# One decode-and-prompt step of a four-mixer trunk: the samples' state outputs as eight full matmuls a layer in place of 32 quarter ones

## What is computed

```python
def step(s, inp):
    u_, wk_, qk_, qh_, kt_, gl_ = inp
    w = u_ - jnp.einsum('bhcd,bhde->bhce', wk_, s)
    o = jnp.einsum('bhcd,bhde->bhce', qh_, s) + jnp.einsum('bhij,bhje->bhie', qk_, w)
    s = jnp.exp(gl_)[..., None, None] * s + jnp.einsum('bhcd,bhce->bhde', kt_, w)
    return s, o
```

## Time and profile before

| | us |
|---|---|
| runs of the kernel before | 1393.62, 1399.95, 1400.35 |
| median | 1399.95 |
| profiled execution | 1395.48 |
| span of its profile | 1393.7 |
| TensorE busy in it | 1273.7 (91%) |
| VectorE busy | 922.9 (66%) |
| ScalarE busy | 730.6 (52%) |
| mean granted TensorE clock | 0.932 of full |

### The profile page before, as it was taken

The page is one execution under the profiler, slowest core; times in us unless marked ns, Lnnn a source line. Parts: engine busy times, 40 slices in busy tenths (PEclk is TensorE's granted clock), DMA queues, the critical chain, the costliest instruction groups (busy, mean ns, idle before and its releaser), DMA issues.

```text
span 1393.7 us, 24010 instructions
## 1 busy us (share of the span) xinstructions
PE 1273.7 (91%) x9815; PEld 1086.3 (78%) x9815; DVE 922.9 (66%) x1546; ACT 730.6 (52%) x1190; POOL 10.0 (1%) x22
## 2 busy tenths in 40 slices
PE   4999898887999998998898788999999999999994
PEld 3899756666999997998666556788878887888874
DVE  1674635724555545676457437998899799979995
ACT  2567222204444444573122115887778778877772
POOL 0000000000000000000000000000000000000000
PEclk8999968698999999999866799999999999999998
DMA  9535358653443453456265431998899889979980
GB/s 388 232 146 208 128 186 327 213 215 121 182 182 144 167 190 129 178 181 219 61 231 183 182 121 61 337 389 306 317 343 386 308 318 346 378 285 337 367 347 33
DMA packets 30325, 326.66 MB, mean 234 GB/s; under 512 B 6018, under 2 KB 6530, under 8 KB 8066
## 3 DMA queue, kind: packets, MB, share of 16 engines
q1 hardware_dynamic: 28738, 319.17, 61.1%
q0 software_dynamic: 1472, 5.89, 1.1%
HBM read 319.15 MB, written 5.89 MB: 233 GB/s over the span
## 4 chain that ended last, share of the span: by engine, by line
PE 82%; DVE 9%; DMA 3%; ACT 3%; issue 3%; SPq 0%; DVEq 0%; POOL 0%; ACTq 0%; POOLq 0%
PE bank L751 19%; PE bank L752 18%; PE bank L753 18%; PE bank L1136 4%; DMA ring<-in_w_ada 3%; PE bank L671 3%; PE bank L807 2%; PE bank L1230 2%; PE bank L703 1%; PE bank L648 1%; PE bank L1258 1%; DVE low L1902 1%; PE bank L693 1%; PE bank L774 1%; PE bank L1009 1%
## 5 line engine op out<-in xcount | busy, mean ns | idle before, releaser
L2425 DVE TENSOR_TENSOR low<-ring,w_high 128x1024 fp32r<-128x1024 f32 x352 | 401.7, 1172 | 41.7 <-ACT w_high L1777 32.9
L1777 ACT ACTIVATE w_high<-ring 128x1024 fp32r<-128x1024 f32 x352 | 355.3, 1021 | 50.5 <-PE bank L753 49.9
L751 PE MATMUL bank<-w_high,hcH 128*128 128x512 f32 x448 | 178.1, 398 | 1.5 <-DVE low L2425 1.3
L753 PE MATMUL bank<-low,hcH 128*128 128x512 f32 x448 | 175.3, 391 | 0.0
L752 PE MATMUL bank<-w_high,hcL 128*128 128x512 f32 x448 | 175.1, 391 | 0.0
L1399 ACT ACTIVATE arena<-bank 128x264 f32<-128x264 f32 (+8 forms) x128 | 51.7, 406 | 135.2 <-PE bank L648 53.9
L751 PE MATMUL bank<-pH,win_high 128*128 128x264 f32 x416 | 120.2, 289 | 2.5 <-issue 2.0
L752 PE MATMUL bank<-pH,low 128*128 128x264 f32 x416 | 118.1, 284 | 0.0
L753 PE MATMUL bank<-pL,win_high 128*128 128x264 f32 x416 | 117.9, 283 | 0.0
L751 PE MATMUL bank<-hH,w_high 128*128 128x264 f32 x352 | 101.1, 287 | 4.9 <-DVE low L2302 4.9
L1399 ACT ACTIVATE w_high<-ring 128x1024 fp32r<-128x1024 f32 (+1 forms) x76 | 71.5, 945 | 63.3 <-PE bank L753 63.3
(11 more groups left out here) (396 smaller groups left out, 2382.9 us busy)
## 6 DMA issues: line engine op xcount, KB each, us to landing
ring<-in_moe_gu SPq DMA_DIRECT2D x56, 2048.0 KB, 8.5
ring<-in_moe_down SPq DMA_DIRECT2D x32, 1792.0 KB, 7.9
ring<-in_w_ada SPq DMA_DIRECT2D x24, 2048.0 KB, 8.9
ring<-in_w_in SPq DMA_DIRECT2D x16, 1536.0 KB, 6.6
ring<-in_ffn_gu SPq DMA_DIRECT2D x11, 2048.0 KB, 7.9
ring<-in_ffn_down SPq DMA_DIRECT2D x8, 1408.0 KB, 5.9
ring<-in_w_out SPq DMA_DIRECT2D x4, 2048.0 KB, 8.3
ring<-in_cache_fox_k SPq DMA_DIRECT2D x32, 128.0 KB, 3.0
```

Source lines behind the costliest of these rows:

```text
L751: mm(out, wh, xh, start=start, stop=False)
L753: return mm(out, wh, xl, start=False, stop=stop)
L1777: A_(split(w_high), src, ACT.Copy).then_inc(sem("w_high_ready"), 1)
L2425: TT(piece_view(t, e_slot(e, i), ring_low)[0], src, split(w_high), ALU.subtract).then_inc(sem("w_low_ready"), 1)
```

## The change

A new tile `qm`, cleared once at the start, holds for each sample, each t and each of two halves a query column that is zero in the partitions of the other head. VectorE fills it with two copies a layer (`own_queries`, ahead of `delta_decay`). `state_outputs` then makes one call for each sample: both of the sample's tiles (128 partitions by 128 columns, four heads) are stationary, and its four query columns move. The result has four columns for each sample in bank 5, of which each head's own output stands in one half of the partitions of one column; ScalarE picks these out with four copies in place of one.

```diff
--- before.py
+++ after.py
@@ -229,6 +229,7 @@
         sxy = sb("sxy", [P, NS])
         rounds = sb("rounds", [P, 1], I32)
         mrow = sb("mrow", [P, P])
+        qm = sb("qm", [P, NS, 2, 2])
 
         ARENA = 25360
 
@@ -1002,12 +1003,8 @@
             def state_outputs():
                 o.need("gst_ready")
                 b = fill(5, "oTs_copied")
-                for t in range(2):
-                    for r in range(2):
-                        q = slice(r * HD, (r + 1) * HD)
-                        for i in range(NS):
-                            ins = mm(b[q, t * NS + i:t * NS + i + 1], gst[q, 2 * i + t, :],
-                                     act[q, t, SEQ + i:SEQ + i + 1], start=True, stop=True)
+                for i in range(NS):
+                    ins = mm(b[:, 4 * i:4 * i + 4], gst[:, 2 * i:2 * i + 2, :], qm[:, i, :, :], start=True, stop=True)
                 ins.then_inc(sem("oTs_done"), 1)
 
             def query_rows():
@@ -1653,7 +1650,11 @@
                                  "v_copied")
                     elif n == 5:
                         o.need("oTs_done")
-                        copy(oT[:, :, SEQ:NT], bank[5][:, 0:2 * NS].rearrange("p (t b) -> p t b", t=2), "oTs_copied")
+                        own = bank[5][:, 0:4 * NS].rearrange("p (b c) -> p c b", c=4)
+                        for t in range(2):
+                            for r in range(2):
+                                o.go(A_(oT[r * HD:(r + 1) * HD, t, SEQ:NT], own[t * HD:(t + 1) * HD, 2 * t + r, :],
+                                        ACT.Copy), "oTs_copied" if t + r == 2 else None)
                     elif n == 6:
                         o.need("yA_gated")
                         o.go(A_(sq[:, 0:2, :], yA[:, :, :], ACT.Square), "head_squares")
@@ -1820,6 +1821,7 @@
                 o.settle()
 
             vs(ve.memset(epsc[:, :], EPS))
+            vs(ve.memset(qm[:, :, :, :], 0.0))
             ve.wait_ge(sem("x_landed"), 16)
             vs(ve.memset(sq[:, 0, 0:1], 0.0), "x_whole")
 
@@ -2154,7 +2156,14 @@
                         v(STT(yA[:, t, SEQ:NT], act[:, 6 + t, SEQ:NT], dcol[:, l, t:t + 1],
                               yd16[:, :].rearrange("p (b t) -> p t b", t=2)[:, t, :], ALU.mult, ALU.add))
 
+                def own_queries():
+
+                    for r in range(2):
+                        q = slice(r * HD, (r + 1) * HD)
+                        v(CP(qm[q, :, :, r], act[q, 0:2, SEQ:NT].rearrange("p t b -> p b t")))
+
                 def delta_decay():
+                    own_queries()
                     vs(TT(g4, g4, spread_bt(2), ALU.mult), "tmpA_free")
                     kbc = act[:, 2:4, SEQ:NT].rearrange("p t b -> p b t").unsqueeze(3).broadcast_to([P, NS, 2, HD])
                     v(TT(b4, g4, kbc, ALU.mult), "Sk_ready")
```

## The result

Over 20 executions of each, the changed kernel took 1401.76 us in the median (1395.43 to 1409.99) and the kernel before 1397.1 us. The recorded ratio, an estimate of its own and not the quotient of the two medians (1.0033), is 1.0048, with a 95% interval of 1.0031 to 1.0064: slower by 4 to 9 us, where 2.9 us less were forecast, and outside the range given. Slow executions, more than 1.5% above the fastest of the same kernel (in the experiments five of the kernel before and one of another), are left out of every mean in this document. The profiled execution took 1401.70 us, its span 1399.9 us, and its mean granted clock was 0.928 (before: 1395.48, 1393.7 and 0.932).

What follows compares the result with a forecast made beforehand. TensorE was taken to bound the kernel, at 82% of the chain that ended last. Savings of 1.44 us (layer 0) and 1.46 us (layer 1), together 2.90, came off a base of 1397.7: 1394.8 us, range 1389 to 1400.5.

Steps and rivals of the forecast that it cites:

- the one on VectorE: VectorE's two copies per layer, 0.33 us, hidden in idle time, and one clearing at the start: no cost.
- The range's own terms: Whole time: 1391.4 to 1398.2, layer 0's bounds (0.2 down, 0.7 up), some 2 us spread each side.
- TensorE's term: State output block: 3.20 to 1.76 us in layer 0, 5.71 to 3.44 in layer 1; saves 1.44 and 1.46.
- the ceiling of 1.46 us: Layer 1: VectorE's idle time before the cache bias, taken as the most that a shorter block can save there.
- the sum: Both layers' savings on TensorE, 1.44 + 1.46 = 2.90 us, with nothing paid back elsewhere.
- The rival that the clock is lost further on: Layer 1 after the cache bias: extra TensorE idle keeps half clock, costing 3.36 us; 1398.2 us, chance 0.15.
- The winning rival: Layer 0 after the block: full clock stays up, saving 3.36 us more; 1391.4 us, chance 0.15.
- The overlap of quarters: State output block: by the skill's page four quarter matmuls cost about one full one, saving 0; the prediction went by the rows.
- The copies of VectorE and ScalarE: Around the block: VectorE's two, 0.33 us a layer, and ScalarE's four, at most 0.54 us more, fit in waits: nothing.

Runs made afterwards that it cites:

- the shift alone: Kernel before plus one unused tile of 128 bytes per partition where the change puts its query tile, no instruction differing; ratios 1.0066 and 1.0038 against the kernel before.
- Quarters in turn: Kernel before with two loops swapped in both layers, so consecutive quarter matmuls go to the two diagonal quarters alternately; ratios 1.0006 and 0.9992 against the kernel before.

## Why the prediction was wrong, point by point

- **The step that failed** is the one on VectorE: "The one clearing of the query tile stands at the start, ahead of VectorE's wait for the input: nothing." The tile was costed by its instructions alone, and no step asked what lies behind it in memory. It measured +6.55 us in the expert stage of the profile, and 7.2 us on the whole time (the shift alone). Without that term the forecast could not be right in sign. (The range's own terms add up to 1400.9 at the top, not 1400.5; 1401.76 lies above both.)
- **TensorE's term was right.** Forecast 1.76 us for the block in layer 0 at full clock, traced 1.88; 3.44 us at half clock, traced 3.6. Layer 1 was cut at the ceiling of 1.46 us, and its idle time went to nothing, with VectorE's passes over the first cache late next, as said. In layer 0 VectorE's idle time was to fall to about 2.6 us and fell to 0.60, since the clock stayed full behind the block.
- **That the sum arrives, "with nothing paid back", was wrong.** At equal half clock the change is worth 3.3 us at the old layout and 3.9 us at the moved one. But with the new block TensorE spends 11 to 17 us more at half clock, and with the tiles at their old places the kernel is level with the one before. The rival that the clock is lost further on had the mechanism, but one place and one price (3.36 us in layer 1, 0.15); that place did fall in the profile (19.58 us for 16.22). Over many executions the added half clock took, at 0.30 us for each, about all of the saving; where in the kernel it arises was not traced.
- **The winning rival** came true only in part: the clock stayed full up to 262 us in layer 0 and the bias came 4.23 us earlier. It had fallen at 268 us, and by 684 us nothing was left.
- **The overlap of quarters** was rightly not counted on for eight quarters in a row through one place. Quarters in turn do overlap (2.0 us), so the old block could be shortened without the change.
- **The copies of VectorE and ScalarE** cost nothing that shows. VectorE's two copies took 0.36 us a layer (0.33 forecast), and its wait before head 4's scores fell from 0.95 to 0.53 us in layer 0 and from 1.36 to 0.74 in layer 1, more than the "0.33 us and no more" that was put down. ScalarE's four copies took 0.76 us. In layer 0 they did not end before TensorE's transposes, as they should have: these ended at 250.92 + 0.38 = 251.30, and ScalarE's next copy came right behind the four, without its old wait of 0.62 us. TensorE did not wait for it.

```profile
250.96 0.76 ACT L1656 ACTIVATE arena<-bank 64x8 f32<-64x8 f32 x4 [1.56 <-PE bank L1007]
251.75 0.49 ACT L1396 ACTIVATE arena<-bank 128x384 f32<-128x384 f32 x1
```

What stays open is why the shorter block goes with more half clock. The amount of TensorE's work does not order the kernels (half clock above the kernel before beside them: 5.9 us with the block left out, 6.7 with half of it, 18.7 and 12.2 with the eight matmuls, 21.6 with them made twice), though with standard errors of 4 to 5 us no neighbours in this list are told apart. Which layer it comes from, and which property of the block decides, was not settled.

## What to carry to other kernels

A new tile is a change to every tile allocated behind it: read the start addresses of the hot operands before and after, and put a small tile where nothing lies behind it, or pad it so that the large ones keep their multiples of 256 bytes. Test such a change by moving the tiles alone, without its instructions; that run costs one line and separates layout from work. A saving of some us on a chain whose clock varies is to be weighed over many executions together with their granted clock, since one trace showed 4 us gained and then lost again in places that the change does not touch.

## What had not been expected of the hardware

- The start of an operand's tile within 256 bytes has a price on matmuls of 512 moving columns: 130.7 us for a pair of experts at a multiple of 256 or of 1024, 131.4 at 64 off, 132.5 at 128 off; 131.3 with the moving tile alone 128 off, and 132.7 with what lies behind it 128 off.
- The feed-forward part of layer 0, with 264 moving columns, hardly pays it. Its matmuls of `hH` with `w_high`, both tiles 128 off after, have a mean of 288 ns for 287 before. There `w_high` is the stationary tile; the slices of the moving `hH` follow each other at 264 x 4 = 1056 bytes, so most of them start off a multiple of 256 in either kernel, and the comparison tells little of the moving operand. Whether the 264 columns or something else makes the difference was not tested (the page's costliest groups, x352; first the kernel before):

```profile
L751 PE MATMUL bank<-hH,w_high 128*128 128x264 f32 x352 | 101.1, 287 | 4.9 <-DVE low L2302 4.9
```

```profile
L752 PE MATMUL bank<-hH,w_high 128*128 128x264 f32 x352 | 101.4, 288 | 4.9 <-DVE low L2311 4.9
```

- One program's executions differ by 19 us (1387.4 to 1406.9 over the 158 of the kernel before), and most of that goes with the granted clock: they had 166 to 236 us at half clock, with some 0.3 us of time for each.
